# Identity matmuls in three of TensorE's waits, and ScalarE's table load and five small transfers moved

## The chip, the cores and the metric

The kernel runs on one core of one Trainium2 chip. The metric is the device time of one execution in microseconds, as the median of several runs. The core has TensorE (PE; its weight loads are PEld), VectorE (DVE), ScalarE (ACT), GpSimd (POOL) and SyncE (SP). Transfers are issued here from two queues, SyncE's and ScalarE's, and carried by 16 DMA engines.

## What is computed

Two layers over 256 tokens of 1024 values, float32. Each layer adds a mixer and then a mixture of experts to x; a last RMSNorm ends it.

```python
for i in range(DEPTH):                      # DEPTH = 2
    h = rms_norm(x, norm_mix_g[i])
    if i % 2 == 0:
        mix = s5_mixer(h, ...)              # state-space scan in chunks of 64, GELU, gated linear unit
    else:
        mix = diff_attention(h, w_qkv, lq1, lk1, lq2, lk2, subln_g, w_o, ...)
    x = x + mix
    x = x + hier_moe(rms_norm(x, norm_ffn_g[i]), ...)   # 4 groups of 8 experts, 2 of one group chosen
return rms_norm(x, final_norm_g)

# in diff_attention
lam = exp(sum(lq1 * lk1)) - exp(sum(lq2 * lk2)) + lambda_init
attn = p[:, :, 0] - lam * p[:, :, 1]
```

The two layers' experts hold some 200 MB of weights, which are read once each.

## The kernel before

Each engine has its own program, written out by hand, and the engines meet at semaphores. Order within an engine is the order of the code. SyncE issues all large loads: the weights go in units of 2 MB through eleven slots of SBUF, and before each load SyncE waits until the slot's last unit has been used (`freed`, L490).

The time runs through these stages, by the profile: the state-space layer (to about 160 us), the experts of layer 0 (to 380), attention (to 530) and the experts of layer 1 (to 780), then the last norm.

Three places matter here.

*Place 1.* TensorE ends `drive(3)` (L1735, the scan's inputs of the last quarter, 64 columns) and comes to `y(0)`, the first output of the scan. Its first matmuls (L1791) wait for `f_ready`, which ScalarE's copies in `own(0)` (L730) raise, and for the scan's inputs; those of L1795 wait for VectorE's `state`. y(0) to y(1) go on to ScalarE's GELU and to the transposes of L1803. y(2) and y(3) come later.

*Place 2.* When the last pass of layer 0's experts has scattered its result into PSUM (`scat1`), ScalarE copies half of x out (L618, `x_late`) and VectorE the other half (L1470, `x_new`). ScalarE then runs a Sqrt on a constant (L619), only so that its Sqrt table is loaded there. TensorE transposes x (`turn_tile(2, 0)`, L1640), ScalarE and VectorE copy the transposes to hT (L646, L1059), and TensorE's projections of q, k and v follow: `project(tt, c)` for two tiles of tokens and six weight units (L1992, 8 matmuls of 128x512 each). The order on TensorE is project(0, 0), turn_tile(2, 1), project(0, 1), `turn_qk(0, 0)` (L2002), project(0, 2), turn_qk(0, 1) and so on. turn_qk waits until VectorE has applied the rotary positions (`rotate`, L1505 to L1509).

Ahead of its first `rotate`, VectorE makes the scalar lam of the reference: it waits for `s_att`, that is for the four lambda vectors and the subln gain, multiplies and sums (L1487, L1488), ScalarE takes the exponential (L905), and VectorE ends it (L1490 to L1492). ScalarE issues these five transfers (L583, called from L900 and L901) after its last pass of the experts of layer 0, before `norm_raw`. Each is spread over the 128 partitions.

SyncE's program at that time: six units of qkv and two of w_o (L416), then a wait for `x_new` and `x_late`, the gain of the final norm (L529), then the experts of layer 1 (L437). Their first unit waits for `qkv_done` 7, which is raised by project(1, 0).

*Place 3.* In the last pass of layer 1's experts TensorE ends the down projections (L1956) and comes to the last `scatter_parts` (L1921): 12 bfloat16 matmuls of 128x512, 6 for each tile of tokens, which wait for `split_ready`. Between them ScalarE and VectorE split the result y in three bfloat16 parts (L1452, L886, L889, L891, L1457, L894, L1461). `y0_ready` is raised when VectorE has read PSUM bank 6 (L1452). Behind the scatter come the last norm's squares (L593), roots (L637), scales (L1028) and the output's transfers (L537).

Of the kernel before, what the change touches and what calls it, by code (L numbers as in the profile page):

```python
# [18 lines left out]
ACT = mybir.ActivationFunctionType  # L19
AX = mybir.AxisListType  # L20

P = 128
# [44 lines left out]
C_TURN = C_UPTO + 9 * 8  # L67
# [53 lines left out]
def build(nc, a, out):  # L121
    with ExitStack() as ctx:
        ctx.enter_context(nc.allow_non_contiguous_dma(reason="short runs of the small parameters"))

        def sb(name, shape, dt=F32):
            return ctx.enter_context(nc.sbuf_tensor(name, shape, dt))

        def sem(name):
            return ctx.enter_context(nc.semaphore(name))
# [7 lines left out]
        con = sb("con", [P, C_N])  # L137
# [3 lines left out]
        small = sb("small", [P, 64])  # L141
        cum = [sb(f"cum{l}", [P, 17 + 9 * l], I32) for l in range(2)]
        work = sb("work", [P, 18560])
        ps = ctx.enter_context(nc.psum_tensor("ps", [P, 8, 512], F32))

        ident = con[:, C_ID:C_ID + P]
# [105 lines left out]
        def low_half(half):  # L252

            return yy[:, 512 * half:512 * half + 256].bitcast(BF16)
# [15 lines left out]
        lam4 = pv_rest[:, 0:256].rearrange("p (n c) -> p n c", n=4)  # L270
        soft_row = pv_rest[:, 0:128].rearrange("p (b n) -> p b n", b=2)
        subg = pv_rest[:, 256:384]
# [12 lines left out]
        s_con, s_x, s_lam, s_bc, s_router, s_gain0, s_gains, s_gain, s_att = (  # L285
            sem(n) for n in ("con_in", "x_in", "lam_in", "bc_in", "router_in", "gain0_in", "gains_in", "gain_in", "att_in"))
# [33 lines left out]
        down_done, y0_ready, y1_ready, scat0, scat1 = (  # L320
            sem(n) for n in ("down_done", "y0_ready", "y1_ready", "scat0", "scat1"))
# [29 lines left out]
        def landing(i):  # L351

            slot, _, count = plan[i]
            return landed[slot], count
# [14 lines left out]
        def passes_through(eng, l, q=NQ - 1):  # L369

            return eng.value_load(cum[l][0:1, NQ + q + 1:NQ + q + 2], min_val=1, max_val=MOST)

        def passes_since(eng, q):

            return eng.value_load(cum[1][0:1, 17 + q:18 + q], min_val=0, max_val=MAXPASS * NQ)
# [32 lines left out]
        def _(sp):  # L408
# [117 lines left out]
                    columns(unit(0, NQ, c), a["attn_w_o"][0], 512 * (c - 6), False)  # L526
            sp.wait_ge(x_new, 2)
            sp.wait_ge(x_late, 2)
            sp.dma_start(gains[:, 1, :], a["final_norm_g"].partition_broadcast(P)).then_inc(s_gain, 16)  # L529
            for i in range(6 * NQ):  # L530
                freed(unit(1, 0, i))
# [49 lines left out]
        def _(act):  # L581
            def dma(dst, src, s):
                act.dma_start(dst, src).then_inc(s, 16)  # L583
# [7 lines left out]
            def square(tt, src):  # L591

                act.activation(xr[:, tt, :, :].rearrange("p k q -> p (k q)"), src, ACT.Square,  # L593
                               accum_out=small[:, 8 + tt:9 + tt]).then_inc(squares, 1)
# [18 lines left out]

            def norm_raw(first):

                act.wait_ge(scat1, first)
                for tt in range(TT):
                    act.copy(x[:, tt, 512:1024], ps[:, 2 * tt + 1, :]).then_inc(x_late, 1)  # L618
                act.activation(small[:, 40:41], con[:, C_TURN:C_TURN + 1], ACT.Sqrt)  # L619
                keep_tile(2, 0)  # L620
                for tt in range(TT):
                    act.wait_ge(x_new, tt + 1)
                    act.wait_ge(x_late, tt + 1)
                    square(tt, x[:, tt, :])
                    root_tile(2, tt)
                    if tt == 0:
                        keep_tile(2, 1)
# [6 lines left out]
            def root_tile(i, tt):  # L634

                act.wait_ge(var_ready, VARS[i] + tt)
                act.activation(small[:, 12 + tt:13 + tt], small[:, 10 + tt:11 + tt], ACT.Sqrt).then_inc(root_ready, 1)  # L637

            def keep_tile(i, tt):

                gain = gq[:, 2, :] if i == 2 else ffg[:, i // 2, :]
                if i == 1 and tt == 0:
                    act.wait_ge(s_router, 160)
                act.wait_ge(hT_psum, TURNED[i] + tt)
                for k in range(4):
                    ins = act.activation(hT[:, k, tt * P:(tt + 1) * P], ps[:, TURN_AT[i][tt], P * k:P * k + P], ACT.Copy,  # L646
                                         scale=gain[:, k:k + 1])
                ins.then_inc(hT_ready, 1)
# [247 lines left out]

            total = moe(0)

            for n, name in enumerate(("q1", "k1", "q2", "k2")):
                dma(lam4[:, n, :], a["attn_lambda_" + name][0].partition_broadcast(P), s_att)  # L900
            dma(subg, a["attn_subln_g"][0].partition_broadcast(P), s_att)  # L901
            norm_raw(total + 1)

            act.wait_ge(lam_sum, 1)
# [716 lines left out]
        def _(pe):  # L1621
            mm = pe.matmul
# [12 lines left out]
            def turn_tile(i, tt):  # L1635

                for k in range(KD):
                    if k % 4 == 0:
                        pe.wait_ge(x_late if k else x_new, tt + 1)
                    ins = pe.transpose(ps[:, TURN_AT[i][tt] + k // 4, P * (k % 4):P * (k % 4) + P], x[:, tt, P * k:P * k + P], ident)  # L1640
                ins.then_inc(hT_psum, 1)
# [16 lines left out]
            def logits(l, tt):  # L1658
# [8 lines left out]
                if tt == TT - 1:  # L1667
                    ins.then_inc(logits_done, 1)

            for first in (turned, down_done, scat0, scat1):  # L1670
                pe.sem_inc(first, 1)
            pe.wait_ge(s_con, 16)
# [50 lines left out]
            def drive(o):  # L1723

                pe.wait_ge(w1T_ready, 4 * o + 4)
                if o == 0:
                    pe.wait_ge(u4_ready, 16)
                    pe.wait_ge(bbar_ready, 1)
                else:
                    pe.wait_ge(u_in[o], 16 * SB)  # L1730
                if o == 2:
                    pe.wait_ge(v_in, 4)
                for r in range(OCT):
                    for i in range(2):
                        ins = mm(ps[:, V_AT[o] + r // 4, P * (r % 4) + 64 * i:P * (r % 4) + 64 * i + 64], W1T[o % 2][:, i, r, :],  # L1735
                                 U4[:, OCT * o + r, :], start=True, stop=True)
                    if r % 4 == 3:
                        ins.then_inc(v_done, 1)

            def taps(o):  # L1740

                pe.wait_ge(w2_ready, o + 1)
                if o == 0:
                    pe.wait_ge(block_b, 4)
                    pe.wait_ge(w1_ready, 8)
                for quad in range(2):
                    for lo, hi, tap in ((0, PC, Cb), (PC, P, W2)):
                        for i in range(2):
                            for r in range(4):
                                pair = OCT * o + 4 * quad + r  # L1750
                                at0 = P * (pair // 4 % 4)
                                ins = mm(ps[32 * r:32 * r + 32, 6 + pair // 16, at0 + lo:at0 + hi], BB[i][:, pair, :], tap[:, i, pair, 0:hi - lo],
                                         start=(i == 0), stop=(i == 1))
                ins.then_inc(k_done, 1)
# [22 lines left out]
            taps(0)  # L1777
            taps(1)
            drive(3)

            def y(o):

# [61 lines left out]
            def moe(l):  # L1844
# [70 lines left out]
                def scatter_parts(m):  # L1915

                    pe.wait_ge(split_ready, 2 * m + 2)
                    for tt, scat in enumerate((scat0, scat1)):
                        for half in range(2):
                            for i, v in enumerate((y_hi, y_mid, None)):  # L1920
                                ins = mm(ps[:, 2 * tt + half, :], selT[:, P * tt:P * tt + P], low_half(half) if i == 2 else v[:, 512 * half:512 * half + 512],  # L1921
                                         start=False, stop=(i == 2), skip_group_check=True)
                        ins.then_inc(scat, 1)
# [5 lines left out]
                for q in range(NQ):  # L1929
# [3 lines left out]
                    with pe.Fori(0, passes) as p:  # L1933
                        n = n0 + p
# [17 lines left out]
                        for half in range(2):  # L1952
                            for k in range(2):
                                for e in range(QE):
# [3 lines left out]
                                             start=(k == 0), stop=(k == 1))  # L1958
                            ins.then_inc(down_done, 1)
                        if l == 0:  # L1960
                            for half, (y_here, scat) in enumerate(((y0_ready, scat0), (y1_ready, scat1))):
# [3 lines left out]
                                             yy[:, 512 * half:512 * half + 512], start=False, stop=True, skip_group_check=True)  # L1965
                                ins.then_inc(scat, 1)
                if l == 1:
                    scatter_parts(passes_since(pe, NQ))

            turn_raw(1, 0, 0)  # L1970
# [6 lines left out]
            normed_rows(0, 0, 0)  # L1977
            logits(0, 1)
            moe(0)

            def project(tt, c):
# [87 lines left out]
                        ins.then_inc(wo_done, 1)  # L2069

            turn_tile(2, 0)
            pe.wait_ge(hT_ready, 5)
            pe.wait_ge(hT_late, 5)
            project(0, 0)
# [66 lines left out]
            normed_rows(1, 0, 0)  # L2141
            logits(1, 1)
            moe(1)


# [19 lines left out]
```

## Time and profile before

| | |
|---|---|
| median of 3 runs | 791.15 us (791.02 to 795.64) |
| profiled execution | 791.36 us, span 789.6 us |
| TensorE busy | 682.4 us, 86% |
| VectorE busy | 299.4 us, 38% |
| ScalarE busy | 249.2 us, 32% |
| mean granted clock of TensorE | 0.954 of 2.4 GHz |
| HBM | 235.21 MB read, 300 GB/s over the span |
| chain that ended last, by engine | PE 55%, SPq 15%, DMA 12%, DVE 10%, ACT 5% |

The span goes from the first to the last instruction; the execution's own time is 1.8 us more. Busy TensorE isn't TensorE at its peak: matmuls are pipelined, and the clock is granted at 1.00 (2.4 GHz) or 0.50 (1.2 GHz); a value between is a mean over a stretch. A matmul in float32 shows as two rows. In a timeline, the brackets give the engine's idle time before a row and what ended it. "SPq" and "ACTq" are transfers being issued: the second number is how long the issue held the engine's queue, not how long the transfer took.

### The profile page before, as it was taken

Reading aid. Unit: us, or ns where it says so; the run is one execution under the profiler, and the core shown is the slowest. Engines: PE = TensorE matmul, PEld = TensorE weight load, DVE = VectorE, ACT = ScalarE, POOL = GpSimd, SP = SyncE. Lnnn points to the kernel's source line nnn. Section 1 sums busy time; section 2 is a strip of 40 time slices with the busy share of each in tenths; the row PEclk is TensorE's granted clock in tenths of the full one; section 3 lists DMA queues with packets and bytes.
Section 4 is the critical chain, followed back from the end, with each engine's and each line's share of the span. In section 5 each row is a group of like instructions: output and inputs, shape, how many; then the busy total and the mean of one; then the engine's idle time right before and its main releaser. Section 6 shows DMA issues by size and latency. Waiting matters only on the chain.

```text
span 789.6 us, 16128 instructions
## 1 busy us (share of the span) xinstructions
PE 682.4 (86%) x6390; PEld 403.8 (51%) x6404; DVE 299.4 (38%) x776; ACT 249.2 (32%) x579; POOL 35.3 (4%) x36
## 2 busy tenths in 40 slices
PE   4898999989977577576899999898989999985994
PEld 4787654555534244244444444555655655652562
DVE  6899761171111011011232534736334433331334
ACT  6687433261111011011311314534233322321224
POOL 1770000000000000000000000000000000000000
PEclk9999999999998887899999999999999999997998
DMA  9335609879999999999990565048999933999981
GB/s 251 112 134 193 186 8 412 346 299 381 419 421 419 422 420 420 422 420 409 381 382 22 213 220 206 0 172 327 424 419 421 420 163 114 423 419 421 419 336 54
DMA packets 64767, 237.92 MB, mean 301 GB/s; under 512 B 24432, under 2 KB 24640, under 8 KB 40128
## 3 DMA queue, kind: packets, MB, share of 16 engines
q1 hardware_dynamic: 63808, 236.82, 75.8%
q8 instruction: 43, 0.70, 0.4%
q10 hardware_dynamic: 896, 0.24, 0.1%
q14 instruction: 20, 0.16, 0.1%
HBM read 235.21 MB, written 1.84 MB: 300 GB/s over the span
## 4 chain that ended last, share of the span: by engine, by line
PE 55%; SPq 15%; DMA 12%; DVE 10%; ACT 5%; issue 2%; DVEq 0%; ACTq 0%
SPq L437 12%; PE ps L1901 12%; PE ps L1992 10%; PE ps L1956 6%; PE ps L1816 6%; PE ps L1881 5%; DMA hT<-in_moe_w_up 4%; DMA ring<-in_moe_w_up 4%; PE ps L1921 4%; DMA ring<-in_moe_w_down 3%; SPq L435 2%; PE ps L2055 2%; PE ps L2066 2%; ACT work L730 2%; PE ps L1964 1%
## 5 line engine op out<-in xcount | busy, mean ns | idle before, releaser
L1901 PE MATMUL ps<-ring,work 128*32 128x256 f32 x1504 | 125.7, 418 | 35.8 <-DMA ring<-in_moe_w_up 12.6
L1901 PEld LDWEIGHTS ps<-ring,work 128*32 128x32 f32 x1504 | 70.6, 120 | 77.9 <-issue 57.6
L1901 PE MATMUL ps<-work 128*32 128x256 f32 x864 | 90.4, 412 | 18.6 <-DMA ring<-in_moe_w_up 6.1
L1433 DVE TENSOR_TENSOR work<-ps,work 128x256 f32<-128x256 f32 x21 | 12.9, 614 | 190.9 <-PE ps L1901 190.9
L1956 PE MATMUL ps<-ring,work 128*32 128x512 f32 x464 | 70.7, 611 | 6.5 <-issue 5.8
L1901 PEld LDWEIGHTS ps<-work 128*32 128x32 f32 x864 | 49.2, 119 | 49.7 <-issue 33.0
L1881 PE MATMUL ps<-work,xr 128*128 128x128 bf16 x736 | 66.4, 219 | 0.7 <-DVE work L1342 0.6
L1881 PE MATMUL ps<-work 128*128 128x128 bf16 x368 | 63.9, 219 | 0.0
L1881 PEld LDWEIGHTS ps<-work,xr 128*128 128x128 bf16 x736 | 57.6, 98 | 8.9 <-issue 3.3
L1992 PE MATMUL ps<-ring,hT 128*128 128x512 f32 x128 | 58.1, 608 | 1.8 <-ACT hT L646 1.8
L1816 PE MATMUL ps<-ring,work 128*128 128x512 f32 x128 | 56.2, 595 | 0.9 <-ACT work L730 0.5
L1921 PE MATMUL ps<-work 128*128 128x512 bf16 x154 | 37.0, 390 | 6.0 <-DVE work L1461 4.0
L870 ACT ACTIVATE work<-ps 128x256 f32<-128x256 f32 x21 | 13.2, 631 | 88.9 <-PE ps L1901 88.9
L1992 PEld LDWEIGHTS ps<-ring,hT 128*128 128x128 f32 x128 | 24.3, 195 | 30.3 <-issue 27.9
L1816 PEld LDWEIGHTS ps<-ring,work 128*128 128x128 f32 x128 | 23.8, 190 | 29.8 <-issue 27.7
L1901 PE MATMUL ps<-hT,work 128*32 128x256 f32 x160 | 39.0, 400 | 0.0
L1956 PE MATMUL ps<-work 128*32 128x512 f32 x176 | 36.3, 595 | 1.8 <-issue 1.2
L1956 PEld LDWEIGHTS ps<-ring,work 128*32 128x32 f32 x464 | 18.2, 112 | 35.7 <-issue 34.7
L877 ACT COPY work<-ps 128x256 f32<-128x256 f32 x13 | 4.8, 372 | 99.5 <-PE ps L1912 99.5
L1881 PEld LDWEIGHTS ps<-work 128*128 128x128 bf16 x368 | 36.0, 98 | 0.0
L855 ACT ACTIVATE work<-ps,work 128x128 f32<-128x128 f32 x92 | 26.2, 368 | 25.5 <-PE ps L1881 25.5
L1921 PEld LDWEIGHTS ps<-work 128*128 128x128 bf16 x168 | 15.7, 100 | 27.6 <-issue 7.6
(338 smaller groups left out, 1070.5 us busy)
## 6 DMA issues: line engine op xcount, KB each, us to landing
ring<-in_moe_w_down SPq DMA_DIRECT2D x22, 2048.0 KB, 24.1
ring<-in_moe_w_gate SPq DMA_DIRECT2D x21, 2048.0 KB, 19.6
ring<-in_moe_w_up SPq DMA_DIRECT2D x16, 2048.0 KB, 30.2
work<-in_moe_w_up SPq DMA_DIRECT2D x12, 2048.0 KB, 20.7
work<-in_moe_w_gate SPq DMA_DIRECT2D x9, 2048.0 KB, 28.9
work<-in_moe_w_down SPq DMA_DIRECT2D x8, 2048.0 KB, 23.8
ring<-in_ssm_w_glu SPq DMA_DIRECT2D x4, 2048.0 KB, 9.0
ring<-in_attn_w_qkv SPq DMA_DIRECT2D x4, 2048.0 KB, 27.5
```

The source lines that it names most:

```text
L435: sp.dma_start(halves[slot_of(i)][e], src[:, e, :]).then_inc(here, 16)
L437: sp.dma_start(places[slot_of(i)].rearrange("p (e n) -> p e n", e=2), src).then_inc(here, 16)
L730: act.copy(dst[:, :, r, 32 * (3 - j):P], kps[:, :, 0:32 * (j + 1)]).then_inc(f_ready, 1)
L855: ins = act.activation(xg[:, k, :], ps[:, 5, P * (k - 4):P * (k - 4) + P], ACT.Copy, scale=gq[:, 2 * l + 1, k:k + 1])
L1816: ins = mm(ps[:, GLU_OUT[n] + half, :], gT[:, k, tt * P:(tt + 1) * P], win[u][:, k, :], start=(k == 0), stop=(k == KD - 1))
L1881: ins = mm(ps[:, 4 + k // 4, P * (k % 4):P * (k % 4) + P], parts[i][:, tt, k, :], sel[:, tt, :], start=(tt == 0 and i == 0), stop=(tt == T ...
L1901: ins = mm(ps[s, 6 + j // 2, 0:256], xg[:, k, s], pairs[slots[e // 2]][e % 2][:, k, :], start=(k == 0), stop=(k == KD - 1))
L1921: ins = mm(ps[:, 2 * tt + half, :], selT[:, P * tt:P * tt + P], low_half(half) if i == 2 else v[:, 512 * half:512 * half + 512], start=Fal ...
L1956: ins = mm(ps[s, 6 + half, :], hidT[:, P * k + 32 * e:P * k + 32 * e + 32], downs[slots[e // 2]][e % 2][:, k, 512 * half:512 * half + 512] ...
L1992: ins = mm(ps[:, qkv_bank(tt, c), :], hT[:, k, tt * P:(tt + 1) * P], win[slot][:, k, :], start=(k == 0), stop=(k == KD - 1))
L2055: ins = mm(ps[:, bank, :], oT[:, k, 0:P], win[slot][:, k, :], start=(k == 0), stop=(k == KD - 1))
L2066: ins = mm(ps[:, 2 + c, :], oT[:, k, P:2 * P], win[slot_of(unit(0, NQ, 6 + c))][:, k, :], start=(k == 0), stop=(k == KD - 1))
```

## The change

- TensorE gets a helper, `keep_clock(bank, n)`, which multiplies the identity by the first 512 columns of the constants n times, each time into one PSUM bank that nobody reads afterwards. It is called with n = 7 before y(0), n = 3 between turn_tile(2, 0) and project(0, 0), and n = 7 before the last scatter. At the last it first waits for `y0_ready` of the last pass, since it writes bank 6.
- ScalarE's Sqrt on a constant, and so its table load, moves ahead of the wait for `scat1` in `norm_raw`.
- The five transfers of lambda vectors and subln gain move from ScalarE's queue to SyncE's, behind the units of w_o and the wait for `x_new` and `x_late`, ahead of the final gain.

```diff
--- before.py
+++ after.py
@@ -526,6 +526,9 @@
                     columns(unit(0, NQ, c), a["attn_w_o"][0], 512 * (c - 6), False)
             sp.wait_ge(x_new, 2)
             sp.wait_ge(x_late, 2)
+            for n, name in enumerate(("q1", "k1", "q2", "k2")):
+                sp.dma_start(lam4[:, n, :], a["attn_lambda_" + name][0].partition_broadcast(P)).then_inc(s_att, 16)
+            sp.dma_start(subg, a["attn_subln_g"][0].partition_broadcast(P)).then_inc(s_att, 16)
             sp.dma_start(gains[:, 1, :], a["final_norm_g"].partition_broadcast(P)).then_inc(s_gain, 16)
             for i in range(6 * NQ):
                 freed(unit(1, 0, i))
@@ -613,10 +616,10 @@
 
             def norm_raw(first):
 
+                act.activation(small[:, 40:41], con[:, C_TURN:C_TURN + 1], ACT.Sqrt)
                 act.wait_ge(scat1, first)
                 for tt in range(TT):
                     act.copy(x[:, tt, 512:1024], ps[:, 2 * tt + 1, :]).then_inc(x_late, 1)
-                act.activation(small[:, 40:41], con[:, C_TURN:C_TURN + 1], ACT.Sqrt)
                 keep_tile(2, 0)
                 for tt in range(TT):
                     act.wait_ge(x_new, tt + 1)
@@ -896,9 +899,6 @@
 
             total = moe(0)
 
-            for n, name in enumerate(("q1", "k1", "q2", "k2")):
-                dma(lam4[:, n, :], a["attn_lambda_" + name][0].partition_broadcast(P), s_att)
-            dma(subg, a["attn_subln_g"][0].partition_broadcast(P), s_att)
             norm_raw(total + 1)
 
             act.wait_ge(lam_sum, 1)
@@ -1667,6 +1667,11 @@
                 if tt == TT - 1:
                     ins.then_inc(logits_done, 1)
 
+            def keep_clock(bank, n):
+
+                for _ in range(n):
+                    mm(ps[:, bank, :], ident, con[:, 0:512], start=True, stop=True)
+
             for first in (turned, down_done, scat0, scat1):
                 pe.sem_inc(first, 1)
             pe.wait_ge(s_con, 16)
@@ -1777,6 +1782,7 @@
             taps(0)
             taps(1)
             drive(3)
+            keep_clock(7, 7)
 
             def y(o):
 
@@ -1965,6 +1971,8 @@
                                              yy[:, 512 * half:512 * half + 512], start=False, stop=True, skip_group_check=True)
                                 ins.then_inc(scat, 1)
                 if l == 1:
+                    pe.wait_ge(y0_ready, passes_through(pe, l))
+                    keep_clock(6, 7)
                     scatter_parts(passes_since(pe, NQ))
 
             turn_raw(1, 0, 0)
@@ -2069,6 +2077,7 @@
                         ins.then_inc(wo_done, 1)
 
             turn_tile(2, 0)
+            keep_clock(0, 3)
             pe.wait_ge(hT_ready, 5)
             pe.wait_ge(hT_late, 5)
             project(0, 0)
```

On TensorE, place 2, before (L1640 turn_tile, L1992 project, L2002 turn_qk, with the semaphores they wait for):

```order
L1640 MATMUL ps<-con,x 128x128 [waits x_late]
L1640 MATMUL ps<-con,x 128x128 x3
L1992 MATMUL ps<-ring,hT 128x512 [waits landed2,hT_late,hT_ready]
L1992 MATMUL ps<-ring,hT 128x512 x7
L1640 MATMUL ps<-con,x 128x128 [waits x_new]
L1640 MATMUL ps<-con,x 128x128 x3
L1640 MATMUL ps<-con,x 128x128 [waits x_late]
L1640 MATMUL ps<-con,x 128x128 x3
L1992 MATMUL ps<-ring,hT 128x512 [waits landed4]
L1992 MATMUL ps<-ring,hT 128x512 x7
L2002 MATMUL ps<-con,work 128x128 [waits qkv_kept]
```

and now, where L1673 is the helper, L2000 project and L2010 turn_qk:

```order
L1640 MATMUL ps<-con,x 128x128 [waits x_late]
L1640 MATMUL ps<-con,x 128x128 x3
L1673 MATMUL ps<-con 128x512 x3
L2000 MATMUL ps<-ring,hT 128x512 [waits landed2,hT_late,hT_ready]
L2000 MATMUL ps<-ring,hT 128x512 x7
```

Three matmuls, which wait for nothing, stand between the transposes and the first projection; the rest keeps its order.

On SyncE, between the units of attention's weights and those of layer 1's experts, the difference (L416 `columns`, L529 and L532 the final gain, L437 the experts' units):

```order
 L416 DMA ring<-in_attn_w_o 128x8x512 x2
-L529 DMA gains<-in_final_norm_g 128x1024
+L530 DMA work<-in_attn_lambda_q 128x64
+L530 DMA work<-in_attn_lambda_k 128x64
+L530 DMA work<-in_attn_lambda_q 128x64
+L530 DMA work<-in_attn_lambda_k 128x64
+L531 DMA work<-in_attn_subln_g 128x128
+L532 DMA gains<-in_final_norm_g 128x1024
 L437 DMA ring<-in_moe_w_gate 128x2x2048 x2
```

The five transfers came from ScalarE's program and stand now behind both units of w_o.

## Rows read from the trace of the kernel before

**Rows 1.** Busy time by stretch: us, then each engine's, clock, DMA share, GB/s:

```profile
core 0: us, PE busy (x) PEld busy (x) DVE busy (x) ACT busy (x) POOL busy (x), PEclk, DMA share, GB/s
...
416.00:418.00 2.00, 2.00 (x6) 0.95 (x5) 0.59 (x1) 0.00 (x0) 0.00 (x0) 1.00 0.13 51
418.00:438.00 20.00, 19.22 (x61) 8.69 (x59) 1.94 (x4) 4.76 (x19) 0.00 (x0) 1.00 0.00 0
```

**Rows 2.** Timeline of SyncE's and ScalarE's issues: start us, us held, what:

```profile
376.61 0.37 ACTq L583 DMA_DIRECT2D work<-in_attn_lambda_q  x1
...
391.24 10.51 SPq L416 DMA_DIRECT2D ring<-in_attn_w_o  x2
401.85 5.18 SPq L529 DMA_DIRECT2D gains<-in_final_norm_g  x1
438.13 0.37 SPq L437 DMA_DIRECT2D ring<-in_moe_w_gate  x1
```

**Rows 3.** Timeline of TensorE at place 1: start us, us, instructions, [idle before]:

```profile
70.93 3.76 PE L1735 MATMUL ps<-gains,ring 128*128 128x64 f32 x32
78.52 1.97 PE L1791 MATMUL ps<-work,gains 128*64 128x128 f32 x16 [3.83 <-ACT work L730]
```

**Rows 4.** TensorE by short stretch: busy us, granted clock, DMA share, GB/s:

```profile
75.00:76.00 1.00, 0.00 (x0) 0.79 1.06 410
...
78.50:82.00 3.50, 3.48 (x34) 0.50 1.05 394
...
780.00:782.00 2.00, 2.00 (x6) 0.50 0.00 0
```

**Rows 5.** The chain that ended last, whole span: start us, us, what:

```profile
80.49 2.75 PE ps L1795 x32
83.23 0.87 PE ps L1791 x16
84.11 1.77 PE ps L1795 x32
...
749.57 2.54 PE ps L1921 x11
```

**Rows 6.** The chain again, from 376 to 440 us:

```profile
380.64 1.28 ACT L619
...
383.22 8.59 PE ps L1992 x16
...
399.65 0.66 PE ps L2002 x4
400.30 6.87 PE ps L1992 x16
```

**Rows 7.** DMA from 340 to 440 us: queue shares, then issues, KB, us to landing:

```profile
q10 hardware_dynamic: 720, 0.20, 0.9%
...
ring<-in_attn_w_o SPq DMA_DIRECT2D x2, 2048.0 KB, 19.6
...
gains<-in_final_norm_g SPq DMA_DIRECT2D x1, 512.0 KB, 15.5
...
work<-in_attn_subln_g ACTq DMA_DIRECT2D x1, 64.0 KB, 7.5
```

**Rows 8.** Timeline of VectorE where it reads the lambda vectors:

```profile
395.99 0.29 DVE L1487 TENSOR_TENSOR work<-work 128x128 f32<-128x128 f32 x1
```

**Rows 9.** Timeline at the last scatter:

```profile
779.14 4.02 PE L1921 MATMUL ps<-work 128*128 128x512 bf16 x11 [3.96 <-DVE work L1461]
...
781.52 1.02 ACT L593 ACTIVATE xr<-ps 128x1024 f32<-128x1024 f32 x1 [2.00 <-PE ps L1921]
```

**Rows 10.** Timeline of SyncE's queue where the router's small transfers are issued:

```profile
75.77 3.88 SPq L465 DMA_DIRECT2D ffg<-in_norm_ffn_g  x1
79.70 3.71 SPq L466 DMA_DIRECT2D wr<-in_moe_w_router_group  x1
...
90.08 0.43 SPq L469 DMA_DIRECT2D rb<-in_moe_b_router_expert  x1
```

**Rows 11.** DMA issues of the whole span: KB each, median us to landing:

```profile
rb<-in_moe_b_router_group SPq DMA_DIRECT2D x2, 2.0 KB, 2.7
```

## Prediction

> **What bounds the kernel now.** I read the stretch of attention's projections first, because the change puts waits there. From 418 to 438 us TensorE is busy 19.22 of 20 us while the DMA engines move nothing [rows 1]: the projections have no slack on TensorE, and the weights of layer 1 can't start before these projections free their slots. SyncE's first load of layer 1 is issued at 438.13 [rows 2]. So whatever delays TensorE between 400 and 438 us delays layer 1's weights by as much, and the end with them. Then I read the three places of the change in the timeline, in the chain of waits and by the granted clock, and last SyncE's own queue, because the change also moves five small transfers.
>
> **Place 1, before y(0): 7 identity matmuls.** TensorE's last matmuls before the wait end at 70.93 + 3.76 = 74.69; y(0) starts at 78.52, released by ScalarE's L730, after 3.83 us idle [rows 3]. The granted clock falls from 1.00 to 0.50 (1.2 GHz) in that gap and is at 0.50 from 78.5 to 82 [rows 4]. What this costs: the 16 rows of L1791 take 1.97 us at the low level [rows 3] and 0.87 at the high one, the 32 of L1795 2.75 and 1.77 [rows 5]; together 2.1 us. The filler is not free either. A matmul of 128x512 f32 shows as two rows, and 16 such rows of L1992 take 6.87 us, 0.43 us each [rows 6]; 7 matmuls are 14 rows, 6.0 us. They end at 74.69 + 6.0 = 80.7, 2.2 us after y(0) could start. Sum: +2.2 - 2.1 = +0.1, I take 0. If the clock falls under the filler all the same, then in the 3.5 us for which it is low its rows take twice as long, 1.7 us are lost, and y(0) starts high: +1.6 is the upper bound.
>
> **Place 2, attention's head: 3 identity matmuls, and ScalarE's table load moved.** Before, ScalarE loads its table from 380.64 for 1.28 us, between copying x and copying hT, and the first projection starts at 383.22 and takes 8.59 us where the next ones take 6.87 [rows 6]. After, the table load stands ahead of ScalarE's wait for the last scatter. All that ScalarE has there are the five DMA issues from 376.61 on [rows 2], which go away, so the load is hidden under them, and hT is ready some 0.6 us sooner (the load's 1.28 less the 0.7 by which it overlaps the transposes). The filler's 6 rows take 2.6 us behind TensorE's transposes, which end at about 381.2 (383.22 less its 1.83 us of idle and the drain); so the filler, to 383.8, now releases the projection, 0.6 us later than before, and the projection is 1.7 us shorter. By itself that is -1.1 us. It does not reach the end, for the next reason.
>
> **The five small transfers.** Four lambda vectors and the subln gain (4 x 32 KB + 64 KB) were issued on ScalarE's queue from 376.61, and the last landed 7.5 us after its issue [rows 2, 7]. VectorE reads them in L1487 at 395.99 without waiting [rows 8]. After, they stand on SyncE behind all eight loads of qkv and w_o. SyncE is held at each of these: the two issues of w_o start at 391.24 and take 10.51 us, so what follows is issued at 401.85, where final_norm stands now [rows 2]. That is already 5.9 us too late for VectorE. And being issued is not landing. The second w_o, issued at about 396.5, the middle of that row, lands 19.6 us later, at 416.1; final_norm, 512 KB, lands 15.5 us after 401.85, at 417.35 [rows 7]. So on SyncE's queue a transfer lands behind those ahead of it, and the DMA rate is down to 51 GB/s from 416 to 418 [rows 1]. The packets of ScalarE's queue took 0.9% of 100 us, 0.9 us [rows 7]. So the five land at about 416.1 + 0.9 = **417.0**.
>
> The Trainium skill (DMA: Bandwidth & Descriptors, "Queues, rings and completion order") says that each DMA engine takes the descriptors of one ring in their order and goes round between rings, of which SyncE and ScalarE own one each. The trace agrees: 15.5 us on the one, 7.5 on the other beside the same large loads.
>
> **What queues behind that wait.** L1487 stands ahead of every rotate on VectorE. It starts at 395.99, and TensorE's L2002, which waits for the first rotate, at 399.65: 3.66 us of work of VectorE and ScalarE in between [rows 6, 8]. TensorE has project(0,1) done by then; its next instruction is turn_qk(0,0), L2002, and project(0,2) stands behind it in order. So turn_qk(0,0) moves from 399.65 to 417.0 + 3.66 = 420.7: **+21.0 us**. From 400.30 on the chain is TensorE nearly without a gap, 6.87 us for each projection [rows 6], and nothing there gets shorter when VectorE is late. All weights have landed by then, which helps nothing, since none was waited for.
>
> TensorE idles some 20 us before that, so it starts at the low level again. As in the first projection of before, 8.59 - 6.87 = 1.72 us are lost, and a little in the transposes: **+1.8 us**.
>
> **Place 3, the last scatter: 7 identity matmuls.** TensorE's scatter starts at 779.14 after 3.96 us idle, so the down projections end at 775.2; the scatter's first half ends at 781.5, when ScalarE squares it [rows 9]. The clock is 0.50 from 780 to 782 [rows 4]. The filler waits only for y0, which VectorE has written before the down projections end, so it starts at 775.2 and ends at 775.2 + 6.0 = 781.2, 2.1 us after the scatter could start. At the high level a scatter of 12 matmuls takes 2.54 us [rows 5], its first half 1.3; it ends at 782.5 and not at 781.5: **+1.0 us**. The squares, roots and final scales behind it keep their lengths. Bounds: -1.0, if the filler is over when the split is ready, and +2.6, if the clock falls under it as in place 1.
>
> **Sum.** 0 + 21.0 + 1.8 + 1.0 = +23.8 us on a span of 789.6, so 813.4. The profiled execution took 791.36 us with that span, and the median of the runs is 791.15; on the median the sum is **815.0 us**.
>
> **Rivals.**
> - B: the small transfers are only issued later, and then land as fast as on ScalarE's queue. Five issues from 401.85 at 0.43 us each [rows 10] put the last at 403.7, landed 7.5 us later at 411.2: 5.8 less than the forecast, 809.2 us. Against it stand final_norm's 15.5 us. Chance 0.07. The Trainium skill (the same page, "Issuing engines are not separate DMA queues") says that issuing from several engines saves only the time to initiate a DMA; read alone, that is this rival.
> - C: each small issue is held until one more large load has landed, as at 75.77 and 79.70, where small issues take 3.88 and 3.71 us behind two 2 MB loads, and later ones 0.43 [rows 10]. Then the five are issued at 401.85, 407.0, 412.4, 417.7 and 418.2, each large load 5.2 us apart, and the last lands 2.7 us on, as the router's bias does [rows 11], at about 421.2. That is +4.2 on the forecast, 819.2 us. Against it: those two are made of 4 and 16 byte pieces, many more than these. Chance 0.17.
> - D, the other side, not slower: the small transfers land before VectorE comes for them. Its point is 395.99. Then the sum is 0 - 1.1 + 1.0, 791.0 us. SyncE would have to issue them before about 388.5, and it has two w_o to issue from 391.24 on. Chance 0.02.
> - E: the change does not do what it says, the clock falls under the fillers at places 1 and 3: +1.6 each on the forecast, 818.2 us. For it: in place 1 the clock is at 0.79 on the mean from 75 to 76 [rows 4], so it fell within 1 us or so of the last matmul. Chance 0.08.
> - F: only the clock counts, and fillers and transfers hide. Then 2.1, 1.7 and 1.0 us come back, 786.3 us. It asks that the filler ends inside its wait, 3.83 us in place 1, where it takes 6.0. Chance 0.01. The Trainium skill (TensorE: Matmul & The Clock Gate, "Why this matters for your kernels") advises to leave no long idle gap between bursts of matmuls; taken alone it is this rival.
>
> The forecast itself has 0.65. The range takes in C and E and the upper part of B: 810 to 821; the forecast's own is 813 to 817. A measurement of this kernel can tell about 1%, 8 us, from no change. Faster by over 1%: 0.01, for what I have not seen; within 1%: 0.03 (D, F); slower: 0.96.
>
> **What the profile after will show.** VectorE idle for about 21 us before L1487, released by the DMA of a lambda or of subln; TensorE idle about as long before turn_qk(0,0), and a low clock behind it; SyncE's small issues after the second w_o; layer 1's first load at about 461 and not 438; y(0) at 80.7 with the clock at 1.00; the last scatter at about 804, directly behind the filler. The prediction is wrong if VectorE's wait ends before 412, or if layer 1's first load is late by less than TensorE waited.

## The result and the profile after

The changed kernel takes 816.16 us (median of 4 runs, 814.32 to 816.64), the kernel before 792.0 us in the same comparison (4 runs, 791.02 to 795.64): a ratio of 1.0292, 95% interval 1.0254 to 1.033. The profiled execution took 814.32 us with a span of 812.5, against 791.36 and 789.6 before. The sum of the prediction is a statement on the span (+23.8 us); the span grew by 22.9. In the second comparison of the experiments one of the 19 runs of the kernel before took 3914.76 us, and the ratios there leave it out.

The timeline of the changed kernel, attention's head. First SyncE's queue, then VectorE, then TensorE. Columns: start, length, engine, line, what, and in brackets idle time and what ended it.

```profile
390.25 10.51 SPq L416 DMA_DIRECT2D ring<-in_attn_w_o  x2
400.87 5.23 SPq L530 DMA_DIRECT2D work<-in_attn_lambda_q  x1
406.14 0.55 SPq L530 DMA_DIRECT2D work<-in_attn_lambda_k  x1
...
407.89 1.51 SPq L531 DMA_DIRECT2D work<-in_attn_subln_g  x1
409.44 0.64 SPq L532 DMA_DIRECT2D gains<-in_final_norm_g  x1
459.80 0.38 SPq L437 DMA_DIRECT2D ring<-in_moe_w_gate  x1
...
416.31 0.29 DVE L1487 TENSOR_TENSOR work<-work 128x128 f32<-128x128 f32 x1 [21.62 <-DMA work<-in_attn_subln_g]
...
391.37 7.03 PE L2000 MATMUL ps<-ring,hT 128*128 128x512 f32 x16
419.96 1.11 PE L2010 MATMUL ps<-con,work 128*128 128x128 f32 x4 [21.56 <-DVE work L1509]
```

VectorE comes to lam at 394.69 and stands there for 21.62 us, until the subln gain has landed. Before, the same line started at 395.99 without a wait [rows 8]. TensorE ends project(0, 1) at 398.4 and stands for 21.56 us; turn_qk(0, 0), at L2010 now, starts at 419.96 where it started at 399.65 [rows 6]: 20.3 us. SyncE's first load of layer 1 goes from 438.13 [rows 2] to 459.80: 21.7 us.

The DMA view of 340 to 440 us (KB each, us from issue to landing), to be read beside [rows 7]:

```profile
ring<-in_attn_w_o SPq DMA_DIRECT2D x2, 2048.0 KB, 19.7
gains<-in_final_norm_g SPq DMA_DIRECT2D x1, 512.0 KB, 7.7
...
work<-in_attn_subln_g SPq DMA_DIRECT2D x1, 64.0 KB, 8.4
```

The subln gain takes 8.4 us here and took 7.5 on ScalarE's queue, so by itself its time says little about what it waits for. It was issued at 407.89, and 8.4 us later is 416.3, 1.0 us after the second w_o has landed (issued at 395.47, 19.8 us). The gain of the final norm tells more, as it has the same queue and size before and after. Before, it was issued at 401.85 and landed 15.5 us later, at 417.3; now it is issued at 409.44 and lands 7.7 us later, at 417.1. It came 7.6 us later into the queue and landed at the same time, so what stands ahead of it sets the landing and not its own issue. The chain of waits (start, length, what) has this landing in it, and then TensorE's restart:

```profile
395.47 5.29 SPq L416
...
407.89 8.39 DMA work<-in_attn_subln_g
...
421.08 7.76 PE ps L2000 x16
...
429.28 6.87 PE ps L2000 x16
```

The first projection behind the wait takes 7.76 us, the next 6.87, as all of them did before [rows 6]. The granted clock goes with it. Windows of TensorE in the changed kernel (stretch, its length, busy us, granted clock, DMA share, GB/s):

```profile
78.00:79.00 1.00, 1.00 (x3) 1.00 1.05 403
382.00:383.00 1.00, 1.00 (x4) 1.00 1.05 387
405.00:410.00 5.00, 0.00 (x0) 0.50 1.05 387
420.00:421.00 1.00, 1.00 (x5) 0.50 0.00 0
422.00:424.00 2.00, 2.00 (x5) 0.81 0.00 0
```

Under the fillers of places 1 and 2 the clock stays at 1.00; in the new wait of 21 us it falls to 0.50. It is still there at 420 to 421, and back at 1.00 before 424 (0.81 is the mean of the two levels there).

The timeline of TensorE in the changed kernel at the three places; L1673 is the filler:

```profile
70.28 3.76 PE L1740 MATMUL ps<-gains,ring 128*128 128x64 f32 x32
73.88 6.23 PE L1673 MATMUL ps<-con 128*128 128x512 f32 x14
80.03 1.09 PE L1797 MATMUL ps<-work,gains 128*64 128x128 f32 x16
...
381.05 2.74 PE L1673 MATMUL ps<-con 128*128 128x512 f32 x6
383.63 7.03 PE L2000 MATMUL ps<-ring,hT 128*128 128x512 f32 x16
...
796.88 6.28 PE L1673 MATMUL ps<-con 128*128 128x512 f32 x14
803.21 2.54 PE L1927 MATMUL ps<-work 128*128 128x512 bf16 x11
```

The identity matmuls fill the waits and overrun two of them. At place 1, 14 rows take 6.23 us where the wait was 3.83 [rows 3]; y(0) is shorter (1.09 for 1.97 us), but starts later after drive(3), 9.75 us for 7.59. At place 3 they take 6.28 us where the wait was 3.96 [rows 9]. VectorE ends the split at 799.00 + 1.46 = 800.46, so 2.75 us before the scatter that waits for it starts.

### The profile page after: what moved, and what is told of

Read it like the earlier page. It is cut to its first block, busy times and chain, and to the rows that moved or that the text cites. A ratio compares the mean times of both kernels' runs of the same rounds, so it can differ in the third digit from the quotient of the medians.

```text
span 812.5 us, 16199 instructions
## 1 busy us (share of the span) xinstructions
PE 692.0 (85%) x6424; PEld 408.3 (50%) x6438; DVE 299.5 (37%) x776; ACT 249.5 (31%) x579; POOL 35.3 (4%) x36
## 4 chain that ended last, share of the span: by engine, by line
PE 56%; SPq 25%; DMA 8%; DVE 5%; ACT 3%; issue 2%; DVEq 0%; ACTq 0%
SPq L437 14%; PE ps L1907 11%; PE ps L2000 9%; SPq L416 7%; PE ps L1822 6%; PE ps L1962 6%; PE ps L1887 5%; DMA hT<-in_moe_w_up 3%; DMA ring<-in_moe_w_down 3%; PE ps L1927 3%; SPq L435 3%; PE ps L1693 2%; PE ps L2063 2%; PE ps L2074 2%; PE ps L1673 2%
## 5 line engine op out<-in xcount | busy, mean ns | idle before, releaser
L1907 PE MATMUL ps<-work 128*32 128x256 f32 x864 | 92.3, 413 | 23.4 <-DMA ring<-in_moe_w_up 7.4
L2000 PE MATMUL ps<-ring,hT 128*128 128x512 f32 x128 | 57.5, 603 | 0.0
L1907 PE MATMUL ps<-hT,work 128*32 128x256 f32 x160 | 40.7, 413 | 0.0
L1822 PEld LDWEIGHTS ps<-ring,work 128*128 128x128 f32 x128 | 23.8, 190 | 29.9 <-issue 27.7
L2000 PEld LDWEIGHTS ps<-ring,hT 128*128 128x128 f32 x128 | 24.2, 194 | 28.4 <-issue 28.2
L1887 PEld LDWEIGHTS ps<-work 128*128 128x128 bf16 x368 | 36.0, 98 | 0.0
L1693 PE MATMUL ps<-hT,ring 128*128 128x256 f32 x128 | 29.0, 381 | 0.8 <-ACT work L401 0.8
## 6 DMA issues: line engine op xcount, KB each, us to landing
ring<-in_moe_w_down SPq DMA_DIRECT2D x22, 2048.0 KB, 24.2
ring<-in_moe_w_gate SPq DMA_DIRECT2D x21, 2048.0 KB, 19.7
work<-in_moe_w_down SPq DMA_DIRECT2D x8, 2048.0 KB, 23.8
```

The source lines that it names most:

```text
L1693: ins = mm(ps[:, c // 2, 256 * (c % 2):256 * (c % 2) + 256], win[c // 4][:, k, P * (c % 4):P * (c % 4) + P], hT[:, k, :], start=(k == 0), ...
L1822: ins = mm(ps[:, GLU_OUT[n] + half, :], gT[:, k, tt * P:(tt + 1) * P], win[u][:, k, :], start=(k == 0), stop=(k == KD - 1))
L1887: ins = mm(ps[:, 4 + k // 4, P * (k % 4):P * (k % 4) + P], parts[i][:, tt, k, :], sel[:, tt, :], start=(tt == 0 and i == 0), stop=(tt == T ...
L1907: ins = mm(ps[s, 6 + j // 2, 0:256], xg[:, k, s], pairs[slots[e // 2]][e % 2][:, k, :], start=(k == 0), stop=(k == KD - 1))
L2000: ins = mm(ps[:, qkv_bank(tt, c), :], hT[:, k, tt * P:(tt + 1) * P], win[slot][:, k, :], start=(k == 0), stop=(k == KD - 1))
```

## The experiments

The theory (T) is that of the prediction: on SyncE's queue the five transfers land only with the large loads ahead of them, and everything else is small. Ratios below are to the kernel before, with a 95% interval. The kernel before had a median of 791.68 us (29 runs) beside x1, x2, x4 and x5, and 791.84 (19 runs) beside x3, x6 and x7. Each run has one profiled execution, and all rows are from that one.

**x2: of the change, the five transfers alone.** The kernel before with this edit:

```diff
             sp.wait_ge(x_late, 2)
+            for n, name in enumerate(("q1", "k1", "q2", "k2")):
+                sp.dma_start(lam4[:, n, :], ...).then_inc(s_att, 16)
+            sp.dma_start(subg, ...).then_inc(s_att, 16)
...
-            for n, name in enumerate(("q1", "k1", "q2", "k2")):
-                dma(lam4[:, n, :], ..., s_att)
-            dma(subg, ..., s_att)
             norm_raw(total + 1)
```

> The kernel of before with nothing but the five small transfers moved to SyncE behind w_o. Theory T: nearly all of the loss, VectorE waits some 20 us before L1487, TensorE starts turn_qk(0,0) at about 420 and at the low clock; 791.2 + 21.7 = 813 us. Rival F: well under 810, the rest being the fillers'.

Measured: 812.58 us (4 runs), ratio 1.026 (1.023 to 1.029). Timeline of VectorE and TensorE:

```profile
415.89 0.29 DVE L1487 TENSOR_TENSOR work<-work 128x128 f32<-128x128 f32 x1 [20.80 <-DMA work<-in_attn_subln_g]
...
419.55 1.11 PE L2002 MATMUL ps<-con,work 128*128 128x128 f32 x4 [20.75 <-DVE work L1509]
```

Without any filler the same wait is there, and 20.9 us of the 24.2. The transfers alone make nearly all of the loss.

**x1: all of the change but the transfers.** The changed kernel with the five transfers back on ScalarE's queue ahead of norm_raw:

```diff
             sp.wait_ge(x_late, 2)
-            for n, name in enumerate(("q1", "k1", "q2", "k2")):
-                sp.dma_start(lam4[:, n, :], ...).then_inc(s_att, 16)
-            sp.dma_start(subg, ...).then_inc(s_att, 16)
...
+            for n, name in enumerate(("q1", "k1", "q2", "k2")):
+                dma(lam4[:, n, :], ..., s_att)
+            dma(subg, ..., s_att)
             norm_raw(total + 1)
```

> The changed kernel with the five small transfers back on ScalarE's queue, where they were; the fillers and the table load stay. Theory T (the loss is VectorE's wait for the small transfers, since they stand behind w_o in SyncE's queue): VectorE no longer waits before L1487, turn_qk(0,0) is back at 399 us, and the time is back at 791 to 792.5 us, that is -1.1 at place 2, +1.2 at place 3, with up to +0.9 because ScalarE now has five issues and a table load before the last scatter of layer 0. Rival F (the fillers themselves cost: a contended PSUM or a clock held low elsewhere): the wait is gone but at least 5 us of the 23 stay, 797 or more.

Measured: 792.0 us (12 runs), ratio 1.0006 (0.9993 to 1.002). Timeline of VectorE and TensorE:

```profile
394.70 0.29 DVE L1487 TENSOR_TENSOR work<-work 128x128 f32<-128x128 f32 x1
...
773.46 6.28 PE L1673 MATMUL ps<-con 128*128 128x512 f32 x14
```

lam starts without a wait. Place 3 loses: from the last down projections' start to the end of the last scale are 16.1 us, and 14.9 before. Place 2 gains: from x's copy by VectorE (L1470) to turn_qk(0, 0) are 19.4 us, and 20.1 before. The fillers and the table load together are worth nothing that can be measured. The two parts apart, +20.9 and +0.3, make 21.2 us, and the whole change 24.2. Place 2's 0.7 us, which x1 has and the whole change cannot use, explain a part of that. The rows show another part. The span of the changed kernel is 1.6 us longer than that of x2 (812.5 and 810.9), and this lies at place 3: the last down projections start at 793.31 and 793.41, and from there to the end of the last scale are 16.1 us and 14.4. In x2 the scatter starts at a granted clock of 1.00, which falls some 1 us later; in the kernel before it had fallen already. So place 3 with the filler takes 1.2 us more than in the profiled execution of the kernel before and 1.7 more than in that of x2. The rest is not explained. The profiled execution of the changed kernel, 814.32, was the shortest of its four, the others took 816.1 to 816.6, so its rows miss some 2 us of the median.

**x3: the five transfers on SyncE's queue, but ahead of w_o.** This asks whether it is SyncE's queue or the place in it. The changed kernel with the same lines moved into the loop over the units:

```diff
             for c in range(8):
                 freed(unit(0, NQ, c))
+                if c == 6:
+                    for n, name in enumerate(("q1", "k1", "q2", "k2")):
+                        sp.dma_start(lam4[:, n, :], ...).then_inc(s_att, 16)
+                    sp.dma_start(subg, ...).then_inc(s_att, 16)
```

> The changed kernel with the five small transfers still on SyncE, but ahead of the two loads of w_o and behind the sixth of qkv. Theory T (a transfer lands behind what stands ahead of it in its queue): they land just behind the sixth qkv load, at about 405, 11 us sooner than the 416.3 of the changed kernel; VectorE waits some 10 us in place of 21.6, and the time is 816.2 - 11 = 805 us. Rival B (only the time of issue counts, the landing is 7.5 us on): issued from 390, landed by 400, 800 us or less.

Measured: 806.4 us (4 runs), ratio 1.0188 (1.0157 to 1.0219). Timeline of SyncE and VectorE:

```profile
385.98 5.29 SPq L416 DMA_DIRECT2D ring<-in_attn_w_qkv  x1
391.41 5.14 SPq L525 DMA_DIRECT2D work<-in_attn_lambda_q  x1
...
398.55 0.64 SPq L526 DMA_DIRECT2D work<-in_attn_subln_g  x1
399.22 5.36 SPq L416 DMA_DIRECT2D ring<-in_attn_w_o  x2
...
406.75 0.29 DVE L1488 TENSOR_TENSOR work<-work 128x128 f32<-128x128 f32 x1 [10.89 <-DMA work<-in_attn_subln_g]
```

Two large loads less ahead of them make VectorE's release 9.6 us earlier, and the kernel 9.8 us faster. The issue of the gain moved by about as much, 9.3 us (407.89 to 398.55), and it lands 8.2 us after its issue, so x3 by itself doesn't tell whether the issue or the load ahead decides. It agrees with both: the load ahead of the small ones, the sixth of qkv, issued at 385.98, lands 19.7 us later, at 405.7, and VectorE goes on at 406.75. What tells them apart is the final norm's gain above. What x3 shows is that the place in the queue makes the loss, and that on SyncE's queue even the place ahead of w_o is 10.9 us too late for VectorE. The time stayed 1.4 us above the 805 expected. The 9.6 us didn't reach the end in full in the profiled execution: its span is 7.5 us shorter than that of the changed kernel (805.0 and 812.5), since the first projection behind the wait took 8.98 us here and 7.97 there (rows of the timeline), and the router of layer 0 was slow (more on that under x4). The first lambda was held 5.14 us at its issue, as behind w_o.

**x5: no fillers at all.** The table load stays moved, and the five transfers go on ScalarE's queue again, but at a point where ScalarE would idle, behind the first root in norm_raw. The changed kernel without the three calls of `keep_clock` and with:

```diff
                     if tt == 0:
+                        for n, name in enumerate(("q1", "k1", "q2", "k2")):
+                            dma(lam4[:, n, :], ..., s_att)
+                        dma(subg, ..., s_att)
                         keep_tile(2, 1)
```

> As the kernel with short fillers, but with no filler at all: only the table load ahead of the wait and the five transfers in ScalarE's idle time. Theory T: hT is ready 0.6 us sooner, the clock falls at all three places as before: 790.6 us, 0.6 under before and 4.6 over the short fillers. Rival: the clock is not what made these matmuls slow, and this kernel is as fast as the one with short fillers.

Measured: 790.61 us (12 runs), ratio 0.9977 (0.996 to 0.9994). Timeline of TensorE at places 1 and 2:

```profile
79.32 1.98 PE L1796 MATMUL ps<-work,gains 128*64 128x128 f32 x16 [3.84 <-ACT work L733]
...
383.54 8.83 PE L1997 MATMUL ps<-ring,hT 128*128 128x512 f32 x16 [1.23 <-ACT hT L649]
```

The waits of before are back, and with them the slow matmuls: 1.98 us as 1.97 before, 8.83 as 8.59 [rows 3, 6]. Place 2's wait for hT is 1.23 us and was 1.83. So this is what the table load is worth by itself, about 0.6 us of waiting, and 0.4 us from L1470 to turn_qk(0, 0). The other half of the expectation, that x5 would be 4.6 us above the short fillers of x4, did not come true: x4 has a ratio of 0.9979 for the 0.9977 here, and a median only 0.9 us lower. That the clock makes these matmuls slow is read from the rows, then, and not from the times of x4 and x5.

**x4: fillers that fit.** As x5, but with the calls kept and shortened, so that each ends about when its wait does:

```diff
-            keep_clock(7, 7)
+            keep_clock(7, 5)
...
-                    keep_clock(6, 7)
+                    keep_clock(6, 4)
...
-            keep_clock(0, 3)
+            keep_clock(0, 2)
```

> Fillers of 5, 2 and 4 matmuls in place of 7, 3 and 7, so that each ends before its wait does (4.3 of 3.8 to 4.6 us, 1.7 of 1.8, 3.4 of 3.6), and the five transfers on ScalarE's queue in its idle time between the two tiles of attention's head (before its keep_tile(2, 1)), where nothing is held. Theory T with the sizes read from the traces: place 1 -2.1, place 2 -2.1 (0.4 sooner and 1.7 shorter), place 3 -1.1: 791.2 - 5.3 = 786 us. Rival G (the clock falls in spite of a filler that leaves half a microsecond idle, or the gain of place 1 is lost in the weight-bound stage behind it): 788 to 790 us. If the transfers land after 396, up to 2 us come on top.

Measured: 789.73 us (12 runs, 787.71 to 791.49), ratio 0.9979 (0.9962 to 0.9996). The sum had given 786, that is 5.3 us less than before. The three places give 4.4 of them in the profiled execution. Timeline of TensorE:

```profile
74.54 4.51 PE L1673 MATMUL ps<-con 128*128 128x512 f32 x10
78.98 1.09 PE L1797 MATMUL ps<-work,gains 128*64 128x128 f32 x16
...
158.78 2.60 PE L1665 MATMUL ps<-wr,hT 128*128 128x36 f32 x16 [1.30 <-DVE hT L1059]
161.19 5.47 PE L1654 MATMUL ps<-x,work 128*128 128x512 f32 x6
...
382.88 1.88 PE L1673 MATMUL ps<-con 128*128 128x512 f32 x4
384.59 7.03 PE L2000 MATMUL ps<-ring,hT 128*128 128x512 f32 x16
...
775.98 3.70 PE L1673 MATMUL ps<-con 128*128 128x512 f32 x8
779.84 2.54 PE L1927 MATMUL ps<-work 128*128 128x512 bf16 x11 [0.16 <-issue]
```

Place 1 is 1.4 us shorter than before (from the start of drive(3) to the gated unit 15.26 us, and 16.68), where the sum had 2.1; place 2 is 1.7 us shorter and place 3 1.3 us. But the rows at 158.78 and 161.19, in the router of layer 0, which nobody touched, are longer than they were. Timeline of TensorE in the kernel before:

```profile
160.17 1.95 PE L1665 MATMUL ps<-wr,hT 128*128 128x36 f32 x16 [1.30 <-DVE hT L1059]
161.95 2.82 PE L1654 MATMUL ps<-x,work 128*128 128x512 f32 x6
```

2.60 us for 1.95, and 5.47 for 2.82. The wait in front is 1.30 us in both. Windows of TensorE, in x4:

```profile
160.00:162.00 2.00, 2.00 (x8) 0.50 1.03 434
```

and in the kernel before:

```profile
160.00:162.00 2.00, 1.83 (x17) 1.00 1.01 426
```

The router began 1.4 us earlier than before, and the experts behind it start 1.7 us later (175.80 for 174.10): some 3 us lost again in this run. That is about the size of the shortfall. Whether it happened in all twelve runs, the one trace cannot say.

Nor do the short fillers have to be the cause. Up to this point x3 is the changed kernel, with its long fillers and the same wait, and in the changed kernel's trace the router ran at 1.00. In x3's it did not. Timeline and a window of TensorE in x3:

```profile
159.95 1.95 PE L1666 MATMUL ps<-wr,hT 128*128 128x36 f32 x16 [1.30 <-DVE hT L1060]
161.72 4.52 PE L1655 MATMUL ps<-x,work 128*128 128x512 f32 x6
```

```profile
163.00:166.00 3.00, 3.00 (x4) 0.50 0.98 418
```

In the changed kernel the two rows start at 159.84 and 161.62, 0.1 us earlier, and the second takes 2.82 us. So behind this wait the clock fell in one execution and not in another, in code that is the same up to there. That x4's earlier arrival brought it about is not shown.

**x6: x4 with a filler in the router as well.** If the fall of the clock in the router took the gain of x4, one matmul in that wait should give it back.

```diff
             normed_rows(0, 0, 0)
+            keep_clock(0, 1)
             logits(0, 1)
```

> The kernel with short fillers and one more identity matmul in a fourth wait of TensorE: after normed_rows(0, 0, 0), ahead of logits(0, 1), in the router of layer 0, where TensorE waits 1.30 us and where the profiled execution with short fillers had the clock at 0.50 from 160 to 167 us (it cost some 3 us there; before, the clock stayed at 1.00). Theory C (the gain of place 1 was given back there, because the clock now falls in this wait): the clock stays at 1.00, and the median falls from 789.7 to 787 us or so. Rival: the clock falls all the same or elsewhere, 789 to 790 us.

Measured: 787.72 us (8 runs), ratio 0.9953 (0.9932 to 0.9975). Timeline of TensorE, and under it the window of 160 to 162 us:

```profile
157.81 1.02 PE L1673 MATMUL ps<-con 128*128 128x512 f32 x2
159.28 1.95 PE L1665 MATMUL ps<-wr,hT 128*128 128x36 f32 x16 [0.44 <-DVE hT L1059]
161.06 2.82 PE L1654 MATMUL ps<-x,work 128*128 128x512 f32 x6
```

```profile
160.00:162.00 2.00, 2.00 (x14) 1.00 0.99 418
```

The router's rows have the lengths of before again, and the median is 2.0 us below that of x4, which was measured in another comparison (ratios 0.9953 and 0.9979; the intervals overlap a little, 0.9962 to 0.9975). This is the lowest median of all versions, 4.1 us below the kernel before. That fits the theory; how often the router would have run slow without this filler was not measured.

**x7: x6 without the filler of place 1.** y(0) starts cold again; is that worth something?

```diff
             drive(3)
-            keep_clock(7, 5)
```

> As the kernel with the router's filler, but without the filler at place 1. Theory C: place 1's 2 us come back as a loss, 789 us. Rival (place 1's gain is lost in the weight-bound stage behind it): the same time as with it, 787 us.

Measured: 788.71 us (12 runs), ratio 0.9969 (0.9952 to 0.9985). Window of TensorE:

```profile
80.00:82.00 2.00, 2.00 (x23) 0.50 1.05 400
```

The clock is at 0.50 where y(0) runs, and the median is 1.0 us above x6. Expected were 2 us if place 1 counts in full, and none if it is hidden. The intervals of the two overlap, so the times leave open whether place 1's filler is worth 1 us or nothing. The two traces speak against the rival that the experts of layer 0 hide it: the gated unit starts at 86.70 in x6 and 87.81 in x7, place 2's transposes at 379.47 and 380.53, layer 1's first load at 435.59 and 436.52. The lead of 1.1 us is still 0.9 there. In the experts of layer 1 x6's profiled execution loses it again, as the last down projections start at 770.62 and 770.23; these take 333.0 to 335.0 us from the first load on in the nine traces, whatever the version.

## Why the prediction came out right, point by point

- **Nearly only the transfers count.** Shown by x1 (no difference without them) and x2 (20.9 us of 24.2 with them alone).
- **They land behind the large loads and not soon after their issue.** VectorE was released at 416.31; forecast were 417.0, rival B 411.2, rival C 421.2. The 0.7 us have a cause in the rows: SyncE's queue ran 1 us ahead of before, the first small issue starting at 400.87 and not 401.85. The second of the two issues of qkv from 374 us on had been held 7.46 us, and 8.29 before. The two together take 11.52 us in x1 as well, where ScalarE's queue carries the five transfers, and 10.69 in the changed kernel and in x3. The second w_o then landed at 415.3, 0.8 us earlier than before, and the five 1.0 us behind it, as against the 0.9 taken. What the forecast left out is that transfers taken off ScalarE's queue no longer slow SyncE's issues.
- **Rival C** was right in its first step and wrong in all others: the first small issue was held for 5.23 us, the four behind it for 0.55, 0.64, 0.43 and 1.51. It took the held issues of [rows 10] for a rule; here only the first of the 32 KB issues was held long. (Of the router's issues a third one, at 83.45, was held too, 5.97 us.) Its own sum is also 0.3 us off: 418.2 + 2.7 is 420.9.
- **Rival B** missed the release by 5.1 us (411.2 for 416.31), and 4.2 of them are the issue: the last of the five was issued at 407.89 and not at 403.7, since the first was held. Only 0.9 us are the time to landing, 8.4 for 7.5. What speaks against B's mechanism is the final norm's gain, which was issued 7.6 us later than before and landed at the same time. The forecast did not see the first small issue held either; it went by the landing of w_o, which the hold doesn't move. The Trainium skill (DMA: Bandwidth & Descriptors, "Queues, rings and completion order") says that descriptors of one ring are taken in order; the gain's landing at 417.3 and 417.1 agrees. The Trainium skill (the same page, "Issuing engines are not separate DMA queues") also says that issuing from several engines only saves the time to initiate a DMA, and that this is usually small beside the DMA itself. Here it was not small: SyncE was held 5.23 us at 32 KB, and the last of the five was issued 29.3 us later than on ScalarE's queue (407.89 for 378.56), part of it by its later place in the program.
- **The wait is carried in full to the next stage.** turn_qk(0, 0) is 20.3 us late, layer 1's first load 21.7, the last down projections 21.8. The prediction had said that it is wrong if VectorE's wait ends before 412 or if the first load is late by less than TensorE waits; the wait ended at 416.31, and the load is 21.7 us late for a wait of 21.56, so the second sign was passed by 0.1 us only. The difference of 21.7 and 20.3 is the cold restart: 1.4 us, not 1.8. The step that was mis-sized took over the 1.72 us of the cold projection [rows 6] and added for the transposes. In the changed kernel the transposes (1.11 us for 0.66) and the start of the projection ran low, and the clock was back at some point from 422 to 424; the projection lost 0.9 us.
- **Place 1**: forecast +0.1. From the start of drive(3) to the first matmul of the gated unit are 16.97 us, and 16.68 before: +0.3. The clock did not fall under the filler here nor at place 3, so rival E is out.
- **Place 2**: forecast -1.1, swallowed. The second projection starts at 391.37 (392.52 before), and TensorE then waits for turn_qk all the same. Without the transfers it is -0.7 (x1).
- **Place 3**: forecast +1.0. From the down projections' start to the square are 11.11 us, and 9.91 before: +1.2. The filler runs 0.28 us longer than the 6.0 taken.
- **Sum**: 20.3 + 1.4 + 1.2 = 22.9 us, the smaller differences of places 1 and 2 being contained in the 20.3, against 22.9 on the span. The 23.8 forecast was 0.9 too much there; on the median the 815.0 was 1.2 too low, since the other three runs took some 2 us more than the profiled one. The prediction did not foresee that difference, and no run explains it. That the two errors have opposite signs, and partly cancel on the median, is luck.

Rival F's idea, that keeping the clock up pays, was right in kind and wrong for these lengths. Its 4.8 us need fillers that end inside their waits, and then 4.1 us came (x6), after one more place had been filled. Of these 1.1 us are there without any filler (x5), which leaves 3.0 for the fillers, and the intervals of x5 and x6 overlap.

## What to carry to other kernels

A small transfer takes the place in time of the queue it stands in: before moving one, read which transfers are issued ahead of it on that queue, when the last of them lands, and which engine comes for the data first. A filler in a wait must be shorter than the wait, so multiply its row's length by its count and compare; where it overruns, it costs as much as a cold start or more. And read the granted clock of a short wait in more than one trace before giving its fall a cause: the same wait in the same code ran at 1.00 in one execution and at 0.50 in another.

## What the runs showed of the hardware that was not expected

- The same wait of 1.30 us in front of the same 16 matmuls of 36 columns left the clock at 1.00 in the kernel before and the changed kernel, but in x4 and x3 it fell to 0.50 within some 3 us of the wait's end, in x3 in code that is the changed kernel's up to there. In place 1 it fell within about 1 us of the last matmul [rows 4]. So in this kernel the length of a wait alone does not tell whether the clock falls; what does was not settled.
- After 21.56 us of idle the clock was back at 1.00 by 424 us, at most 4 us after TensorE began at 419.96, with the engine busy all the while. In x3, after 10.84 us of idle, it was at 0.50 from 411 to 415, and TensorE had begun at 410.41.
- Five small transfers on ScalarE's queue (192 KB in all) make SyncE's issue of a 2 MB load at the same time 0.8 us longer: 11.52 us for two in x1, 10.69 in the changed kernel and x3, 10.87 in x2. In x5, where they are issued from some 385 us on, it is the next load that is held longer, 6.00 us at 385.92 for 5.29.
- Of several small issues behind 2 MB loads on SyncE's queue, the first was held 5.23 and 5.14 us (changed kernel, x3), the following ones 0.43 to 1.51.
